# Gathering 56 instead of 64 tokens for each expert of a four-expert unit, with the slots still 64 apart

## What is computed

```python
scores = sigmoid(x2 @ w_router)                  # 288 tokens, 64 experts
...                                              # 4 of 8 groups, then
_, eidx = lax.top_k(where(emask, biased, -inf), 8)
gate = w / sum(w) * 2.5
shared = (silu(x2 @ ws1) * (x2 @ ws3)) @ ws2
# every token goes through its 8 experts:
hdn = silu(x2[tok] @ w1[e]) * (x2[tok] @ w3[e])  # 1024 -> 256
ff  = shared + segment_sum((hdn @ w2[e]) * gate) # 256 -> 1024
x   = layernorm(alpha * x + ff)
```

## Time and profile before

| | |
|---|---|
| time, median of 3 runs | 1609.67 us (1609.35 to 1609.72) |
| the profiled execution: its time | 1609.49 us |
| the profiled execution: its span | 1607.5 us |
| PE busy, share of the span | 1569.8 us, 98% |
| DVE, ACT, POOL busy | 742.2, 569.4, 23.0 us |
| HBM read | 474.88 MB |

### The profile page before, as it was taken

One profiled execution on the slowest core, in us unless ns is written; L12 is line 12 of the kernel. 1 busy time (PEld: TensorE's weight loads), 2 busy tenths in 40 slices (PEclk: granted clock), 3 DMA queues, 4 the chain that ended last, 5 costly groups with the idle time before them and its releaser, 6 DMA issues.

```text
span 1607.5 us, 25611 instructions
## 1 busy us (share of the span) xinstructions
PE 1569.8 (98%) x9496; PEld 1039.8 (65%) x9496; DVE 742.2 (46%) x1528; ACT 569.4 (35%) x1134; POOL 23.0 (1%) x38
## 2 busy tenths in 40 slices
PE   8999999999999999999999999999999999999997
PEld 7978997655454555555588789975555555554554
DVE  5658667333333423332474786662433332333336
ACT  4766434222232223222267564342223222222322
POOL 2000000000000000000010000000000000000000
PEclk9999999999999999999999999999999999999998
DMA  8553356499999999999536434458999999999991
GB/s 232 175 197 105 126 165 242 176 389 405 406 383 411 401 396 408 393 405 393 212 119 207 164 106 139 155 212 322 382 410 397 398 402 403 394 399 409 391 407 42
DMA packets 141588, 477.35 MB, mean 297 GB/s; under 512 B 10052, under 2 KB 74116, under 8 KB 108756
## 3 DMA queue, kind: packets, MB, share of 16 engines
q1 hardware_dynamic: 139760, 473.50, 76.4%
q0 software_dynamic: 1408, 2.85, 0.6%
q10 hardware_dynamic: 356, 0.13, 0.0%
HBM read 474.88 MB, written 1.57 MB: 296 GB/s over the span
## 4 chain that ended last, share of the span: by engine, by line
PE 92%; DVE 4%; ACT 1%; DMA 1%; issue 1%; SPq 0%; DVEq 0%; ACTq 0%
PE ps L943 27%; PE ps L963 14%; PE ps L582 6%; PE ps L583 6%; PE ps L584 6%; PE ps L569 5%; PE ps L984 4%; PE ps L925 4%; PE ps L985 4%; PE ps L926 4%; PE ps L928 2%; PE ps L972 1%; DMA dense<-in_w_in 1%; PE ps L905 1%; PE ps L951 1%; PE ps L725 1%
## 5 line engine op out<-in xcount | busy, mean ns | idle before, releaser
L943 PE MATMUL ps<-experts,xg 128*64 128x512 f32 x2048 | 450.5, 592 | 0.0
L943 PEld LDWEIGHTS ps<-experts,xg 128*64 128x64 f32 x2048 | 147.8, 137 | 290.6 <-issue 289.7
L963 PE MATMUL ps<-experts,hidT 128*64 128x512 f32 x1024 | 233.8, 598 | 1.0 <-ACT hidT L1309 1.0
L582 PE MATMUL ps<-parts 128*128 128x288 f32 x736 | 224.1, 304 | 4.0 <-DVE dense_lo L1438 3.7
L584 PE MATMUL ps<-parts,dense_lo 128*128 128x288 f32 x736 | 217.4, 295 | 0.0
L1765 DVE TENSOR_TENSOR hid<-ps,hid 128x256 f32<-128x256 f32 x64 | 27.2, 425 | 385.1 <-ACT hid L1303 385.1
L1317 ACT ACTIVATE yh<-ps,gsl 128x512 fp32r<-128x512 f32 x128 | 88.0, 687 | 230.0 <-PE ps L963 230.0
L1303 ACT ACTIVATE hid<-ps 128x256 f32<-128x256 f32 x64 | 24.5, 384 | 397.6 <-PE ps L943 397.6
L1295 ACT ACTIVATE xg<-ps,gperm_all 128x256 f32<-128x256 f32 x256 | 130.6, 561 | 63.6 <-PE ps L928 60.0
L1777 DVE SCALAR_TENSOR_TENSOR yl<-ps,gsl,yh 128x512 fp32r<-128x512 f32 x128 | 96.1, 751 | 122.7 <-ACT yh L1317 122.7
L963 PEld LDWEIGHTS ps<-experts,hidT 128*64 128x64 f32 x1024 | 68.2, 136 | 121.0 <-issue 121.0
(11 more groups left out here) (290 smaller groups left out, 2019.5 us busy)
## 6 DMA issues: line engine op xcount, KB each, us to landing
experts<-in_w SPq DMA_DIRECT2D x384, 1024.0 KB, 9.4
dense<-in_w_in SPq DMA_DIRECT2D x33, 1024.0 KB, 5.5
dense<-in_w_br_rnn SPq DMA_DIRECT2D x8, 1024.0 KB, 5.2
dense<-in_w_br_attn SPq DMA_DIRECT2D x8, 1024.0 KB, 5.2
dense<-in_w_out SPq DMA_DIRECT2D x8, 1024.0 KB, 5.2
dense<-in_ws SPq DMA_DIRECT2D x6, 1024.0 KB, 5.5
tok<-in_x_prompt SPq DMA_DIRECT2D x2, 512.0 KB, 4.5
dense<-in_w_in SPq DMA_DIRECT2D x2, 512.0 KB, 7.6
```

The source lines that it names most:

```text
L582: mm(bank[:, 0:T], w_hi[:, k, col:col + P], hi[:, k, :], start=k == 0, stop=False)
L943: last = mm(ps[e % 2 * CAP:(e % 2 + 1) * CAP, 2, :], xg[:, k, e * CAP:e * CAP + CAP], experts[:, e, 0:2, k * DE:k * DE + DE], start=k == 0 ...
L963: last = mm(ps[e % 2 * CAP:(e % 2 + 1) * CAP, 3 + b, :], hidT[:, m, e % 2 * CAP:(e % 2 + 1) * CAP], experts[:, e, 2, m * D + b * 512:m * D ...
```

## The change

CAP becomes 56, and a new constant SLOT = 64 keeps the distance between the slots of two experts wherever tiles are laid out. `oh` is written densely, 4 x 56 = 224 columns, and `gather` moves 224 columns in place of 256. `keep_gathered` reads 224 columns of PSUM and writes them into `xg` as four runs of 56, each at a distance of 64. `gated` writes `og` in the same way. `up`, `down`, `slots_to_tokens` and `combine` keep their shapes. The eight spare slots of each expert in `og` and `xg` are set to zero by two memsets on DVE, once per layer, in the first unit between `keep_low(2)` and `gated`; DVE then waits for its own signal `spare_clear`, and so does PE's first `up`. The tables `iota` and `thr` follow CAP (224 in place of 256 numbers, and 5 in place of 4).

```diff
@@ -50,7 +50,8 @@
 
-CAP = 64
+CAP = 56
+SLOT = 64
 SWAP = (0, 1, 5, 6)
@@ -228,15 +229,15 @@
         xl = sb("xl", [P, NT - 1, D], F32R, scope=s2)
-        oh = sb("oh", [P, NT, QUAD * CAP], F32R, scope=s2)
+        oh = sb("oh", [P, NT, QUAD * SLOT], F32R, scope=s2)
         s2a = ExitStack()
...
         s2a.close()
-        xg = sb("xg", [P, KC, QUAD * CAP], scope=s2)
+        xg = sb("xg", [P, KC, QUAD * SLOT], scope=s2)
         ohT = sb("ohT", [P, 2, T], F32R, scope=s2)
-        og = sb("og", [P, NT, QUAD * CAP], scope=s2)
+        og = sb("og", [P, NT, QUAD * SLOT], scope=s2)
         hid = sb("hid", [P, DE], scope=s2)
-        hidT = sb("hidT", [P, ME, 2 * CAP], scope=s2)
+        hidT = sb("hidT", [P, ME, 2 * SLOT], scope=s2)
         s2b = ExitStack()
@@ -270,6 +271,7 @@
         as_f = lambda x: x.bitcast(F32)
+        in_slots = lambda x, t: x.rearrange(f"p {t} (e s) -> p {t} e s", s=SLOT)
 
@@ -364,6 +366,7 @@
         xg_kept = sem("xg_kept")
+        spare_clear = sem("spare_clear")
         w13_done = sem("w13_done")
@@ -914,7 +917,7 @@
                         for k in (2 * j, 2 * j + 1):
-                            o = ps[:, SWAP[j], k % 2 * 256:k % 2 * 256 + 256]
+                            o = ps[:, SWAP[j], k % 2 * 256:k % 2 * 256 + QUAD * CAP]
                             x = slice(k * P, k * P + P)
@@ -922,10 +925,10 @@
                             for t in range(NT - 1):
-                                mm(o, xh[:, t, x], oh[:, t, :], start=t == 0, stop=False)
-                                mm(o, xl[:, t, x], oh[:, t, :], start=False, stop=False)
-
-                            last = mm(o, xh[:, NT - 1, x], oh[:, NT - 1, :], start=False, stop=True)
+                                mm(o, xh[:, t, x], oh[:, t, 0:QUAD * CAP], start=t == 0, stop=False)
+                                mm(o, xl[:, t, x], oh[:, t, 0:QUAD * CAP], start=False, stop=False)
+
+                            last = mm(o, xh[:, NT - 1, x], oh[:, NT - 1, 0:QUAD * CAP], start=False, stop=True)
                         last.then_inc(xg_full, 1)
@@ -933,6 +936,8 @@
                         pe.wait_ge(xg_kept, n * 4 + 4)
+                    else:
+                        pe.wait_ge(spare_clear, L + 1)
                     pe.wait_ge(hidT_ready, FREE + n * 2 + u)
@@ -940,7 +945,7 @@
                         for e in (2 * u, 2 * u + 1):
-                            last = mm(ps[e % 2 * CAP:(e % 2 + 1) * CAP, 2, :], xg[:, k, e * CAP:e * CAP + CAP],
+                            last = mm(ps[e % 2 * SLOT:(e % 2 + 1) * SLOT, 2, :], xg[:, k, e * SLOT:e * SLOT + SLOT],
                                       experts[:, e, 0:2, k * DE:k * DE + DE], start=k == 0, stop=k == KC - 1)
@@ -960,7 +965,7 @@
                             for e in (2 * u, 2 * u + 1):
-                                last = mm(ps[e % 2 * CAP:(e % 2 + 1) * CAP, 3 + b, :], hidT[:, m, e % 2 * CAP:(e % 2 + 1) * CAP],
+                                last = mm(ps[e % 2 * SLOT:(e % 2 + 1) * SLOT, 3 + b, :], hidT[:, m, e % 2 * SLOT:(e % 2 + 1) * SLOT],
                                           experts[:, e, 2, m * D + b * 512:m * D + b * 512 + 512], start=m == 0, stop=m == ME - 1)
@@ -1292,7 +1297,8 @@
                         for k in (2 * j, 2 * j + 1):
-                            last = activation(xg[:, k, :], ps[:, SWAP[j], k % 2 * 256:k % 2 * 256 + 256], ACT.Identity,
+                            rows = ps[:, SWAP[j], k % 2 * 256:k % 2 * 256 + QUAD * CAP].rearrange("p (e s) -> p e s", e=QUAD)
+                            last = activation(in_slots(xg[:, :, :], "t")[:, k, :, 0:CAP], rows, ACT.Identity,
                                               bias=gperm_all[:, L, 1, k:k + 1], scale=gperm_all[:, L, 0, k:k + 1])
@@ -1747,7 +1753,7 @@
                     b = rank[:, :, bass.ds(i * QUAD, QUAD)].rearrange("p t (e o) -> p t e o", o=1).to_broadcast(shape)
-                    V.tensor_tensor(oh[:, :, :].rearrange("p t (e s) -> p t e s", e=QUAD), a, b, ALU.is_equal)\
+                    V.tensor_tensor(oh[:, :, 0:QUAD * CAP].rearrange("p t (e s) -> p t e s", e=QUAD), a, b, ALU.is_equal)\
                         .then_inc(oh_ready, 1)
@@ -1755,9 +1761,9 @@
                     shape = (P, NT, QUAD, CAP)
-                    a = oh[:, :, :].bitcast(F32).rearrange("p t (e s) -> p t e s", e=QUAD)
+                    a = oh[:, :, 0:QUAD * CAP].bitcast(F32).rearrange("p t (e s) -> p t e s", e=QUAD)
                     b = gate[:, :, bass.ds(i * QUAD, QUAD)].rearrange("p t (e o) -> p t e o", o=1).to_broadcast(shape)
-                    V.tensor_tensor(og[:, :, :].rearrange("p t (e s) -> p t e s", e=QUAD), a, b, ALU.mult).then_inc(og_ready, 1)
+                    V.tensor_tensor(in_slots(og[:, :, :], "t")[:, :, :, 0:CAP], a, b, ALU.mult).then_inc(og_ready, 1)
 
@@ -1841,6 +1847,9 @@
                         dve.wait_ge(xl_ready, (L + 1) * NT)
+                        V.memset(in_slots(og[:, :, :], "t")[:, :, :, CAP:SLOT], 0.0)
+                        V.memset(in_slots(xg[:, :, :], "t")[:, :, :, CAP:SLOT], 0.0).then_inc(spare_clear, 1)
+                        dve.wait_ge(spare_clear, L + 1)
                     gated(q, 0)
```

## The result

The changed kernel takes 1600.69 us, the median of 5 runs (1599.55 to 1601.38), against 1609.67 us. The ratio is 0.9944, with a 95% interval of 0.9933 to 0.9956: between 7.1 and 10.8 us less. The forecast was 1599.5 us.

A forecast was written before the change was run, and what follows sets the result against it. PE, not the weight stream, was taken to bound the expert stage. A gather shorter by 320 ns in each of 32 units gives 10.2 us, other costs nothing: 1599.5 us beside the median, range 1595.0 to 1610.0 us.

The forecast's parts named there:

- a matmul with the same load and a shorter moving operand: L715, whose 111.5 ns was forecast as the gather's new distance, from 119.5: 320 ns a unit, 10.2 us in all.

## What to carry to other kernels

A matmul on a full PE costs the distance to the next. In the float32r matmuls here it was close to the larger of two things: the stream of the columns and the load of the stationary operand. Taking columns away pays only down to where the load takes over, here at about 240 columns of float32r behind a load of 128; beyond that, ask for fewer or smaller loads (half the load took 0.4 us off a unit). A capacity below that point buys no time and only brings a second pass nearer, so take the largest capacity that is as fast (here 60, not 56). And look in the trace for a matmul with the same load and a shorter moving operand: its distance was the forecast. Then look at the matmuls that the change does not touch: here a slower combine took back a tenth of the gain.

## What was not expected

A float32r matmul stands 7.5 to 10 ns over its columns at 2.4 GHz even when its load is small (114.2 ns for 256 columns with a load of 64, and 103.2 ns for 224 with loads of 64 and of 32 alike), and a full load beside it adds some 5 ns at 256 columns, before it becomes the bound.

Ahead of the expert stages, the executions differ from one to the next. In the profiled execution of the changed kernel the first gather began 1.33 us later than before (286.51 against 285.18 us), which hides a part of the gain in its span. The view by stretches has, for two stretches of the kernel before and then for 32 to 40 us of the one after (us, busy time and count of PE, PEld, DVE, ACT and POOL, granted clock, DMA share, GB/s):

```profile
28.00:32.00 4.00, 4.00 (x21) 4.00 (x21) 3.10 (x9) 3.31 (x10) 0.00 (x0) 0.59 0.49 163
...
36.00:40.00 4.00, 3.18 (x24) 3.21 (x25) 3.83 (x9) 0.63 (x1) 0.00 (x0) 1.00 0.85 256
```
```profile
32.00:36.00 4.00, 1.16 (x7) 0.95 (x6) 3.89 (x7) 2.75 (x7) 0.00 (x0) 0.84 0.55 154
36.00:40.00 4.00, 4.00 (x18) 4.00 (x18) 3.62 (x14) 2.00 (x2) 0.00 (x0) 0.50 0.33 110
```

Both executions have a stretch at a low granted clock: the one before from 28 to 32 us, at 0.59, and the one after from 36 to 40 us, at 0.50, the 1.2 GHz level, after a stretch in which PE was busy for 1.16 of 4 us. The run with 256 columns and half the load had the same 1.16 us there, kept 1.00 from its start on, and reached its first gather at 283.67 us, earlier than either. So a microsecond or two of the times seem to belong to where and how long the clock is low; no run was made to test that. The unit's length in the chain is the better measure of a change in the expert stage.
